# Expert-choice threshold search: eight candidates a round on replicated keys

## The reference

```python
logits = jnp.einsum('btd,de->bte', u, router_w).astype(jnp.float32)
aff = jax.nn.softmax(logits, axis=-1)
g, idx = lax.top_k(jnp.swapaxes(aff, 1, 2), cap)
xs = jax.vmap(lambda ub, ib: ub[ib])(u, flat_idx).reshape(B, N_EXPERTS, cap, D)
hid = jax.nn.silu(jnp.einsum('becd,edf->becf', xs, w_gate)) * \
    jnp.einsum('becd,edf->becf', xs, w_up)
ys = jnp.einsum('becf,efd->becd', hid, w_down) * g[..., None].astype(u.dtype)
```

## Time and profile before

| | |
|---|---|
| median of 3 runs | 2634.9 us (2632.45 to 2637.38) |
| the profiled execution, span from first to last instruction | 2631.6 us |
| TensorE busy | 2516.9 us (96%) |
| VectorE busy | 1399.2 us (53%) |
| ScalarE busy | 1195.2 us (45%) |
| GpSimd busy | 193.2 us (7%) |
| chain that ended last | TensorE 95%, VectorE 2%, issue 1%, DMA 1% |
| mean granted clock of TensorE | 0.977 |

### The profile page before, as it was taken

One profiled execution on the slowest core, in us unless ns is written; L12 is line 12 of the kernel. 1 busy time (PEld: TensorE's weight loads), 2 busy tenths in 40 slices (PEclk: granted clock), 3 DMA queues, 4 the chain that ended last, 5 costly groups with the idle time before them and its releaser, 6 DMA issues.

```text
span 2631.6 us, 56446 instructions
## 1 busy us (share of the span) xinstructions
PE 2516.9 (96%) x21262; PEld 2480.1 (94%) x21262; DVE 1399.2 (53%) x2193; ACT 1195.2 (45%) x1813; POOL 193.2 (7%) x189
## 2 busy tenths in 40 slices
PE   7953999999999999999999999999999999999996
PEld 7952999999999999999999999999999999999996
DVE  4556545545464545555454645555454545555474
ACT  5630444444444444444444444444444444444454
POOL 0020000000001000000001000000001000000101
PEclk9975999999999999999999999999999999999998
DMA  6640556656655656556555656656556656556684
GB/s 215 200 140 23 170 192 183 200 169 195 178 178 177 198 182 190 193 174 199 171 188 178 190 190 177 205 174 193 176 179 184 195 177 190 191 176 203 207 312 172
DMA packets 426301, 485.85 MB, mean 185 GB/s; under 512 B 11761, under 2 KB 406497, under 8 KB 426274
## 3 DMA queue, kind: packets, MB, share of 16 engines
q1 hardware_dynamic: 411106, 433.85, 51.7%
q0 software_dynamic: 10560, 34.87, 5.3%
q10 hardware_dynamic: 4608, 16.78, 1.7%
HBM read 443.26 MB, written 42.21 MB: 184 GB/s over the span
## 4 chain that ended last, share of the span: by engine, by line
PE 95%; DVE 2%; issue 1%; DMA 1%; ACT 0%; DVEq 0%; POOL 0%; SPq 0%; POOLq 0%; ACTq 0%
PE bank L1050 91%; PE bank L1055 4%; DVE above L856 0%; DVE above_b L856 0%; DMA nmix<-in_norm_mix 0%; DVE base L863 0%; ACT u_t L604 0%; DMA x_rows<-u_rows,idx 0%; DVE picks L921 0%; DVE pooled_lo L772 0%; DVE pw L799 0%; DVE flips L859 0%; DVE y_rows L1042 0%; ACT junk L700 0%; ACT squares L574 0%
## 5 line engine op out<-in xcount | busy, mean ns | idle before, releaser
L942 DVE TENSOR_TENSOR w_lo<-raw,w_hi 128x1024 fp32r<-128x1024 f32 x765 | 929.7, 1222 | 567.5 <-ACT w_hi L635 564.7
L1050 PE MATMUL bank<-x_hi,w_hi 128*128 128x258 f32 x4096 | 1162.5, 284 | 5.2 <-issue 3.6
L1050 PE MATMUL bank<-x_hi,w_lo 128*128 128x258 f32 x4096 | 1156.1, 282 | 0.0
L1050 PE MATMUL bank<-x_lo,w_hi 128*128 128x258 f32 x4096 | 1156.0, 282 | 0.0
L635 ACT ACTIVATE w_hi<-raw 128x1024 fp32r<-128x1024 f32 x765 | 804.7, 1052 | 300.2 <-PE bank L1050 253.4
L1050 PEld LDWEIGHTS bank<-x_hi,w_hi 128*128 128x128 f32 x4096 | 774.3, 189 | 9.4 <-issue 9.4
L1050 PEld LDWEIGHTS bank<-x_lo,w_hi 128*128 128x128 f32 x4096 | 777.8, 190 | 0.0
L1050 PEld LDWEIGHTS bank<-x_hi,w_lo 128*128 128x128 f32 x4096 | 771.9, 188 | 0.0
L1050 PE MATMUL bank<-hid_hi,w_hi 128*128 128x258 f32 x2048 | 590.4, 288 | 0.0
L1050 PE MATMUL bank<-hid_lo,w_hi 128*128 128x258 f32 x2048 | 579.5, 283 | 0.0
L1050 PE MATMUL bank<-hid_hi,w_lo 128*128 128x258 f32 x2048 | 579.4, 283 | 0.0
(11 more groups left out here) (138 smaller groups left out, 1289.3 us busy)
## 6 DMA issues: line engine op xcount, KB each, us to landing
raw<-in_moe_w_gate SPq DMA_DIRECT2D x128, 1024.0 KB, 5.2
raw<-in_moe_w_up SPq DMA_DIRECT2D x128, 1024.0 KB, 5.2
raw<-in_moe_w_down SPq DMA_DIRECT2D x128, 1024.0 KB, 4.9
h_in<-in_x SPq DMA_DIRECT2D x18, 512.0 KB, 5.6
x_rows<-h_acc ACTq DMA_DIRECT2D x16, 512.0 KB, 5.8
out<-x_rows ACTq DMA_DIRECT2D x16, 512.0 KB, 4.5
h_acc<-h_mid SPq DMA_DIRECT2D x17, 448.0 KB, 5.0
u_rows<-u_out SPq DMA_DIRECT2D x17, 448.0 KB, 3.0
```

Source lines behind the costliest of these rows:

```text
L942: nc.vector.tensor_tensor(w_lo[:, a % 4], quarter_view(a // 2 % 4, a % 2), w_hi[:, a % 4].bitcast(f32), ALU.subtract).then_inc(split_lo, 1)
L1050: return nc.tensor.matmul(dst, lhs, rhs, start=start, stop=stop)
```

## The change

The affinity's bits are split in two halves of 15, and each half becomes an ordinary float key: the high key is the value of the upper bits times 2^15, the low key the lower 15 bits. Each key is written eight times, so that the transposes (now 19 per half, one for each tile) give eight copies of every expert's 2064 keys, on eight partitions: partition (rank, expert). A halo token that belongs to two tiles is copied out once. One candidate for each partition, rank 0 to 7, makes a round of three bits: each partition counts over all 2064 keys, 896 of them by VectorE (`is_ge` with a sum) and 1168 by ScalarE (the sum of Sign of candidate less key). VectorE turns both into a flag of whether at least 258 keys reach the candidate, one bfloat16 matmul adds the eight flags of an expert, and one operation makes the next candidate from the sum and from `ahead`. Five rounds find the high half; the keys are then merged (low key plus high key less the middle of the found step), and five rounds find the low half. The rounds are written out, with no loop on the engine.

The first keys are written by VectorE (10 tiles) and ScalarE (9 tiles), the low ones by GpSimd in five pieces, ahead of `vals`. VectorE copies two banks of transposed high keys out of PSUM and ScalarE three; ScalarE copies all low ones, behind its counts of rounds 2 to 5. The rounding of the first three half pieces goes from behind Silu's table load to a place ahead of Exp's, and a table load for Sign follows Exp. The constants `worth` and `offsets` give way to a smaller `search`.

The core of the diff:

```diff
+KEYS_V = 10
+COUNT_V = 8 * 112
+COUNT_A = T - COUNT_V
...
+    rank = k // NE
+    search = np.zeros((P, 2, ROUNDS + 1))
+    for half, steps in enumerate(STEPS):
+        search[:, half, 0] = rank * steps[0] - UNITS[half] / 2
+        for j, step in enumerate(steps):
+            below = steps[j + 1] if j + 1 < ROUNDS else 0.0
+            search[:, half, j + 1] = rank * (below - step) - step
+    put("search", search)
...
+        def many_keys(i, c0, c1):
+            few = key_bits[:, i].rearrange("p (c e) -> p c e", e=NE)[:, c0:c1, :]
+            return few.unsqueeze(2).broadcast_to([P, c1 - c0, DIGIT, NE])
+
+        def key_columns(i, b):
+
+            if b < 4:
+                pieces = [(bank[:, b, :].rearrange("p (c t) -> p c t", c=4)[:, :, HALO:P - HALO],
+                           key_t[:, i, 448 * b:448 * b + 448].rearrange("p (c t) -> p c t", c=4))]
+            else:
+                pieces = [(bank[:, 4, 0:2 * P].rearrange("p (c t) -> p c t", c=2)[:, :, HALO:P - HALO],
+                           key_t[:, i, 1792:2016].rearrange("p (c t) -> p c t", c=2)),
+                          (bank[:, 4, 3 * P - 40:3 * P], key_t[:, i, 2024:T])]
+            if b == 0:
+                pieces.append((bank[:, 0, 0:HALO], key_t[:, i, 2016:2024]))
+            return pieces
...
+            pool.wait_ge(bits_split, 2)
+            for c0 in range(0, NT, 4):
+                c1 = min(c0 + 4, NT)
+                nc.gpsimd.tensor_copy(key[:, 1, c0:c1], many_keys(1, c0, c1)).then_inc(keyed_p, 1)
...
+            for a in range(3):
+                act.wait_ge(loaded_w[a // 2], 16)
+                nc.scalar.activation(w_hi[:, a], quarter_view(a // 2, a % 2), ACT.Copy).then_inc(split_hi, 1)
+
             nc.scalar.preload_act_table(ACT.Exp)
             act.wait_ge(shifted, 1)
             nc.scalar.activation(lg[:], lg[:], ACT.Exp).then_inc(exped, 1)
 
+            nc.scalar.preload_act_table(ACT.Sign)
+
+            act.wait_ge(bits_split, 1)
+            nc.scalar.activation(key[:, 0, KEYS_V:NT], many_keys(0, KEYS_V, NT), ACT.Copy).then_inc(keyed_a, 1)
+
+            def key_out(i, b):
+                act.wait_ge(key_turned, 5 * i + b + 1)
+                for src, dst in key_columns(i, b):
+                    nc.scalar.activation(dst, src, ACT.Copy).then_inc(key_out_a, 1)
+
+            for b in (2, 3, 4):
+                key_out(0, b)
+            act.wait_ge(key_out_v, 3)
+            act.wait_ge(key_out_a, 4)
+            for half in range(2):
+                if half == 1:
+                    act.wait_ge(merged, 2)
+                for j in range(ROUNDS):
+                    g = ROUNDS * half + j
+                    act.wait_ge(cand_done, g + 1 + half)
+                    nc.scalar.activation(marks_a[:], key_t[:, half, COUNT_V:], ACT.Sign, bias=cand[:, 0:1],
+                                         scale=-1.0, accum_out=signs[:]).then_inc(signed, 1)
+                    if half == 0 and j > 0:
+                        key_out(1, j - 1)
+                if half == 0:
+                    key_out(1, ROUNDS - 1)
...
+            dve.wait_ge(aff_turned, 1)
+            aff_bits = aff[:].bitcast(i32).rearrange("p c e -> p (c e)")
+            nc.vector.tensor_scalar(key_bits[:, 0], aff_bits, -1 << HALF_BITS, None, ALU.bitwise_and)              .then_inc(bits_split, 1)
+            dve.wait_ge(bits_split, 1)
+            nc.vector.tensor_copy(key[:, 0, 0:KEYS_V], many_keys(0, 0, KEYS_V)).then_inc(keyed_v, 1)
+            nc.vector.tensor_scalar(key_bits[:, 1], aff_bits, (1 << HALF_BITS) - 1, None, ALU.bitwise_and)              .then_inc(bits_split, 1)
+            for b in range(2):
+                dve.wait_ge(key_turned, b + 1)
+                for src, dst in key_columns(0, b):
+                    nc.vector.tensor_copy(dst, src).then_inc(key_out_v, 1)
+            steps = const("search").rearrange("p (h j) -> p h j", h=2)
+
+
+            def search(half, j):
+                g = ROUNDS * half + j
+                dve.wait_ge(cand_done, g + 1 + half)
+                nc.vector.tensor_tensor(ahead[:], cand[:], steps[:, half, j + 1:j + 2], ALU.add)\
+                  .then_inc(looked, 1)
+                nc.vector.tensor_scalar(marks_v[:], key_t[:, half, 0:COUNT_V], cand[:, 0:1], None,
+                                        ALU.is_ge, ALU.add, accum_out=count[:]).then_inc(counted, 1)
+                dve.wait_ge(counted, g + 1)
+                nc.vector.tensor_scalar(short[:], count[:], -1.0, CAP - 0.5 - COUNT_A / 2, ALU.mult, ALU.add)\
+                  .then_inc(shorted, 1)
+                dve.wait_ge(shorted, g + 1)
+                dve.wait_ge(signed, g + 1)
+                nc.vector.tensor_scalar(flag[:], signs[:], -0.5, short[:, 0:1], ALU.mult, ALU.is_ge)\
+                  .then_inc(flagged, 1)
+                dve.wait_ge(looked, g + 1)
+                dve.wait_ge(summed, g + 1)
+                nc.vector.scalar_tensor_tensor(out=cand[:], in0=bank[:, 5, 0:1], scalar=STEPS[half][j],
+                                               in1=ahead[:], op0=ALU.mult, op1=ALU.add).then_inc(cand_done, 1)
+
+            nc.vector.tensor_copy(cand[:], steps[:, 0, 0:1]).then_inc(cand_done, 1)
+            dve.wait_ge(key_out_v, 3)
+            dve.wait_ge(key_out_a, 4)
+            for j in range(ROUNDS):
+                search(0, j)
+            dve.wait_ge(cand_done, ROUNDS + 1)
+            link(nc.vector.tensor_scalar(middle[:], cand[:], UNITS[0] / 2, None, ALU.add))
+            link(nc.vector.tensor_scalar(thr_half[:, 0:1], cand[:], UNITS[0] / 2, None, ALU.add))
+            dve.wait_ge(key_out_a, 11)
+            for span in (slice(COUNT_V, T), slice(0, COUNT_V)):
+                nc.vector.scalar_tensor_tensor(out=key_t[:, 1, span], in0=key_t[:, 0, span],
+                                               scalar=middle[:, 0:1], in1=key_t[:, 1, span],
+                                               op0=ALU.subtract, op1=ALU.add).then_inc(merged, 1)
+            nc.vector.tensor_copy(cand[:], steps[:, 1, 0:1]).then_inc(cand_done, 1)
+            dve.wait_ge(merged, 2)
+            for j in range(ROUNDS):
+                search(1, j)
+            dve.wait_ge(cand_done, 2 * ROUNDS + 2)
+            link(nc.vector.tensor_scalar(thr_half[:, 1:2], cand[:], UNITS[1] / 2, None, ALU.add))
+            link(nc.vector.tensor_tensor(thr_bits[:], thr_half[:, 0:1], thr_half[:, 1:2], ALU.bitwise_or))
+            nc.vector.tensor_scalar(thr_diag[:], const("first"), thr_bits[:].bitcast(f32), None, ALU.mult)\
...
-            with pe.Fori(0, PAIRS) as b:
-                pe.wait_ge(counted, 3 * b + 3)
-                mm(bank[:, 5, 0:3], const("same_expert"), count[:], True, True).then_inc(summed, 1)
-            pe.wait_ge(thr_ready, PAIRS + 1)
+            for i in range(2):
+                if i == 1:
+                    pe.wait_ge(key_out_v, 3)
+                    pe.wait_ge(key_out_a, 4)
+                for c in range(NT):
+                    if i == 1 and c % 4 == 0:
+                        pe.wait_ge(keyed_p, c // 4 + 1)
+                    elif i == 0 and c == 0:
+                        pe.wait_ge(keyed_v, 1)
+                    elif i == 0 and c == KEYS_V:
+                        pe.wait_ge(keyed_a, 1)
+                    last = turn_block(bank[:, c // 4, (c % 4) * P:(c % 4 + 1) * P],
+                                      key[:, i, c].rearrange("p r e -> p (r e)"))
+                    if c % 4 == 3 or c == NT - 1:
+                        last.then_inc(key_turned, 1)
+            for g in range(2 * ROUNDS):
+                pe.wait_ge(flagged, g + 1)
+                mm(bank[:, 5, 0:1], same_b[:], flag[:], True, True).then_inc(summed, 1)
+            pe.wait_ge(thr_ready, 1)
...
```

More of the change, by code:

```diff
@@ L42 @@
 SLOT0 = CAP // 2
-NBITS = 30
-PAIRS = NBITS // 2
+DIGIT = 8
+ROUNDS = 5
+HALF_BITS = 3 * ROUNDS
+UNITS = (float(1 << HALF_BITS), 1.0)
+STEPS = tuple(tuple(unit * DIGIT ** (ROUNDS - 1 - j) for j in range(ROUNDS)) for unit in UNITS)
+KEYS_V = 10
+COUNT_V = 8 * 112
+COUNT_A = T - COUNT_V
 LEFT = CAP - 256
@@ L67, in constant_columns @@
                     ("slots", PICKED), ("reset", NE * NT), ("valid", NT), ("valid_m1", NT),
-                    ("tok_hi", NT), ("tok_lo", NT), ("chunk", 1), ("worth", 3 * PAIRS), ("offsets", 4 * (PAIRS + 1))):
+                    ("tok_hi", NT), ("tok_lo", NT), ("chunk", 1), ("search", 2 * (ROUNDS + 1))):
         cols[name] = (at, at + n)
@@ L202, in encoder_kernel @@
         total = sb("total", [P, NT], f32, phase2)
[L203 to L212, removed]
+        aff = sb("aff", [P, NT, NE], f32, phase2)
+        key_bits = sb("key_bits", [P, 2, NT * NE], i32, phase2)
+        key = sb("key", [P, 2, NT, DIGIT, NE], f32, phase2)
+        key_t = sb("key_t", [P, 2, T], f32, phase2)
+        marks_v = sb("marks_v", [P, COUNT_V], f32, phase2)
+        marks_a = sb("marks_a", [P, COUNT_A], f32, phase2)
+        count = sb("count", [P, 1], f32, phase2)
```

(29 more changed lines are left out.)

26 lines of the change are left out of this document (13 added, 13 removed).

## The result

| | before | after |
|---|---|---|
| median | 2634.9 us (2632.45 to 2637.38) | 2618.24 us (2617.05 to 2619.19, 4 runs) |
| span of the profiled execution | 2631.6 us | 2616.1 us |
| `thr_diag` | 231.05 us | 209.19 us |
| first expert product | 258.97 us | 236.82 us |
| from there to the end | 2372.6 us | 2379.2 us |

The ratio is 0.9937 [0.9923, 0.995]: 16.7 us less, where 19.2 were forecast (2615.7). The table shows the two parts that make it up. The search gave 21.9, more than forecast; the experts, which were to take no notice, took 6.6 back.

What follows compares the result with a forecast made beforehand. The serial threshold search (VectorE, TensorE, VectorE) was taken to bound the improvable stretch. A 176.3 + 6.5 + 4.95 + 20.5 + 3.1 + 0.5 put `thr_diag` at 211.85 instead of 231.05: 19.2 less, 2615.7 us; range 2609.5 to 2624.5.

Steps and rivals of the forecast that it cites:

- what a run's time holds around its span: Time outside the profiled execution's span: 3.3 us at the median (2634.9 - 2631.6), left unchanged.
- affinities ready, A: End of `aff`: VectorE's two-SBUF-input L844 to L846 wait for GpSimd's last `w_lo`; 176.3, 2.2 later than before.
- A to the first round: High keys written, 19 transposes at 0.24 us each (4.6), copies out of PSUM; round 1 can start at A + 6.5.
- round 1: First search round: its matmul queues behind the low half's 19 transposes (4.6 us) on TensorE; 4.95 us, not 2.28.
- nine rounds: The other search rounds at 2.28 us each, 20.5 in all; bounds 2.05 to 2.6 a round.
- between the halves: Two small operations 0.4, merge of 1168 and 896 elements 2.6, copy and wake 0.15: 3.1 us.
- rounding and OR: End of the search: rounding, OR and wake, 0.5 us.
- afterwards: After `thr_diag`: thr, slots, list, gather at unchanged cost, TensorE cold before and after; expert stage unchanged.
- Two rows of before: VectorE's `base` (1.54 instead of 0.22) and `aff_top` (1.33), each ending when a GpSimd `w_lo` ends.
- more gain: Rival: A not held up, transposes at 2.4 GHz, or rounds of 2.05; 22 to 26 us gained, 2609 to 2613; chance 0.17.
- my 3.7 from the cast to `iota`: GpSimd's five key copies, 2432 elements at 1.5 ns each: 3.7 us, done before TensorE starts the low-half transposes.
- the rival that needed 11.5 ns an element: Rival "Slower": GpSimd's key copies take 28 us before round 1, cancelling the gain; slower or nothing left, chance 0.07.

Runs made afterwards that it cites:

- the second profile of the kernel: The changed kernel run and profiled again with no edit: 2617.06 us, ratio 0.9926 to the kernel before.
- The shifts: Redundant instructions added to the changed kernel: TensorE 10, 20 or 1 gave 2612.03, 2612.23, 2613.24 us; ScalarE 20 gave 2616.85; old kernel with 76, 77, 78: 2636.14, 2635.33, 2637.34.

## Why the prediction was right

The time was inside the range and 2.5 us from the forecast. Three misjudged terms make that up: 2.7 too much up to `thr_diag`, 6.3 forgotten behind it, and 1.1 too much for what a run's time holds around its span. I took 3.3 from a median (2634.9) and the span of one faster execution (2631.6); after the change the same difference is 2618.24 - 2616.06 = 2.2. That the first and the last hid part of the second is luck.

| step | forecast | measured |
|---|---|---|
| affinities ready, A | 176.3 | 175.79 + 0.48 = 176.27 |
| A to the first round | 6.5 | 182.38 - 176.27 = 6.1 |
| round 1 | 4.95 | 185.23 - 182.38 = 2.85 |
| nine rounds | 20.5 | 2.72 + 3 x 2.22 + 5 x 2.23 = 20.5 |
| between the halves | 3.1 | 197.66 - 194.62 = 3.04 |
| rounding and OR | 0.5 | 209.19 - 208.81 = 0.38 |
| `thr_diag` | 211.85 | 209.19 |
| afterwards | 0 lost | 6.3 lost |

*A.* The mechanism was right and shown: L918 was held until the last `w_lo` ended (175.21, forecast 175.1). Two rows of before, stretched to the end of a GpSimd instruction, were enough to price a third that no row had. That A itself came out to 0.03 is luck: in the seven profiles with `w_lo` in this place it lies between 175.6 and 177.4. The two versions with a late `w_lo` show it from both sides: from L918's start to A it is 173.28 to 176.27 (2.99) with `w_lo` in front, and 173.20 to 174.40 (1.20) with it late. The Trainium skill's rule ("GPSIMD Engine Reference", § 1 Specifications, two SBUF inputs contend) agrees with these rows, and so does the form with one tensor and a pointer, which did not wait. The prediction's reading, that VectorE waits for the running GpSimd instruction, is too wide: it held for GpSimd's two-tensor instructions, and the cast above let `base` through. What I overlooked is that `ahead` has two SBUF inputs as well, and that GpSimd's two `rest` steps now run beside rounds 1 and 2: 0.64 and 0.53 lost in this profile, nothing in the second one of the same kernel. In the sum it was covered, since round 1 was forecast too long.

*Round 1.* The mechanism, the queue of 19 transposes ahead of the first sum, is there: TensorE goes from 182.39 to 184.65 without a break and its sum follows at 184.74. The size was not: 2.26 us, not 4.6, because the clock had risen. I had taken for a rule about transposes. The rival "more gain" named this case as 19 x 0.11 = 2.1 for either set of transposes; the second set gave it. TensorE was hardly late in this profile: `flag` was ready at 184.69, held up by `ahead`. In the second profile of the kernel `ahead` was not held up, and `cand` was idle for 0.75 before it could take the sum, 0.35 otherwise: there the queue of transposes cost 0.4.

*The rounds, the merge, the table.* As worked out from rows of operations of other sizes, to 0.06 a round. Sign and Copy alternated here without a load between them, and GpSimd's five key copies took 2.74 together for 2432 elements (1.13 ns each). The estimate of 2 us from the rate in the Trainium skill ("GPSIMD Engine Reference", § 4.1 Engine selection) is nearer to that than my 3.7 from the cast to `iota`; the rival that needed 11.5 ns an element has no ground left.

*Afterwards: the step that failed.* "The old chain, thr, slots, list, gather, at unchanged cost" held: 209.19 to 236.82 is 27.6, before 27.9. "TensorE is cold there before and after" was too coarse, and that the expert loop keeps its time was taken for granted from the earlier trace rows. Of the 6.6 us between first product and end:

- 1.4 is the first expert (149.45 against 148.08). TensorE enters it at 1.2 GHz in both kernels, but stays there twice as long. Before and after:

```profile
259.00:262.00 3.00, 3.00 (x14) 3.00 (x15) 1.22 (x1) 0.03 (x1) 0.00 (x0) 0.50 0.13 32
262.00:264.00 2.00, 2.00 (x18) 2.00 (x18) 0.00 (x0) 0.36 (x2) 0.00 (x0) 0.98 0.99 322
```

```profile
236.80:242.80 6.00, 5.98 (x28) 5.98 (x29) 1.23 (x1) 0.66 (x3) 0.00 (x0) 0.50 0.52 161
243.00:245.00 2.00, 2.00 (x18) 2.00 (x18) 1.12 (x1) 0.85 (x1) 0.00 (x0) 1.00 0.06 20
```

The products come every 0.21 at the lower level and every 0.12 at the higher, so 3.1 us more of the lower are some 14 products, each 0.09 longer: 1.3. This belongs to no version: over all fourteen profiles the clock rose between 3.1 and 6.2 us after the first product, and the first expert followed it from 148.1 to 149.5.

- 3.9 is the loop's gap, 14 x 0.28. Another 1.8 is a loss of 0.3 in 6 of the 14 turns, which take 147.85 instead of 147.55 (before, all took 147.25); the last expert gave 0.7 back. The shifts show the gap's price, with what part of the 1.8 goes along with it (in their traces 3 turns or fewer are longer): with the gap 2617.1 and 2616.9, without it 2612.0, 2612.2 and 2613.2. Where the 0.3 comes from wasn't tried. The gap is a cost of where the new code's length put the loop, not of the search.

Without the gap and the clock's luck the forecast of 19.2 would have been too small by the 2.7 of round 1 and its neighbours: the versions that differ by a moved loop alone gained 21.7 to 24.1 us.

## What to carry to other kernels

When a stretch on a serial path is shortened, follow it past its end: the longer straight-line code moves every loop behind it, and one moved loop cost here 4 to 5 of 22 us; a try with one redundant instruction in front tells. Where GpSimd works beside a latency-bound chain of VectorE, write its small steps with one SBUF tensor and a pointer scalar, since one of two SBUF tensors waited for the end of any two-tensor GpSimd instruction that was running. A price read from TensorE at the lower clock level need not hold where the change gives it more to do: 19 dense transposes in a row ended here on the other level.

## What the runs showed of the hardware

- VectorE's operations on two SBUF tensors waited for the end of a running two-tensor GpSimd instruction to within 0.1 us: one element took 0.80, 0.69 and 1.58 instead of 0.16, 19 elements 1.96 instead of 0.18. Beside a GpSimd cast one such operation took its ordinary 0.22 and one 0.67. With a pointer scalar, or with one input in PSUM (`cand` at 187.40, beside the first late `w_lo`: 0.16), they did not wait. GpSimd's own operations kept their length (three `w_lo` 6.99 beside the search, 6.97 beside the router).
- TensorE's clock rose from 0.50 to 1.00 towards the end of the first 19 key transposes, after 3.9 us of them at full occupancy. It stayed at 0.50 through the 24 transposes of `x_rows`, which after the change take 6.6 us without a break:

```profile
228.71 6.58 PE L1152 MATMUL bank<-ident,x_rows 128*128 128x128 f32 x24 [8.32 <-DMA x_rows<-u_rows,idx]
```

  One difference that the profile shows: eight of these 24 turn blocks of two rows (of the kernel before: `x_rows 2*128 2x2 f32 x8`), while all the key blocks are 128x128. Whether that is the reason wasn't tried. Nor is the moment fixed: in the ten profiles with the new search the rise came between 1.5 us before the second 19 began and 0.7 us after, and those took 2.26 to 2.59.
- One redundant instruction in TensorE's stream changed the turn of a loop entered 60 us later by 0.28 us, every time, and the kernel by some 4 us (2613.24 against 2616.85 in the same comparison; ten instructions gave 5.0).
